# A two-layer hybrid decoder step: the second layer's gates computed step by step inside the first turn of its main block, instead of in a block of their own

## The reference

```python
def c_mixer(h, s_ssm, s_conv, w_in, conv_w, conv_b, dt_bias, a_log, d_skip, norm_w, w_out):
    proj = h @ w_in
    z, xbc, dt = _split(proj, (D_INNER, SSD_CONV_DIM, SSD_HEADS))
    xbc, conv_new = causal_conv(xbc, s_conv, conv_w, conv_b)
    xbc = jax.nn.silu(xbc.astype(F32))
    ...
    dt = jax.nn.softplus(dt.astype(F32) + dt_bias.astype(F32)).reshape(bsz, L, SSD_GROUPS, SSD_HPG)
    a = -jnp.exp(a_log.astype(F32)).reshape(SSD_GROUPS, SSD_HPG)
    y, s_new = ssd_scan(xs, dt, a, bm, cm, s0)      # decays are exp of cumulative sums of dt * a
    y = y + d_skip... * xs
    y = y * jax.nn.silu(z);  y = _rms(y by group) * norm_w;  return y @ w_out, s_new, conv_new
```

## Time and profile before

| | |
|---|---|
| median of 3 runs | 2226.04 us |
| the profiled execution, whole | 2225.12 us |
| its span, first to last instruction | 2223.7 us |
| PE busy | 2101.4 us, 95% of the span |
| DVE busy, ACT busy | 64%, 45% |
| transfers | 436.97 MB, mean 197 GB/s |
| mean granted TensorE clock | 0.975 of full |

### The profile page before, as it was taken

The page is one execution under the profiler, slowest core; times in us unless marked ns, Lnnn a source line. Parts: engine busy times, 40 slices in busy tenths (PEclk is TensorE's granted clock), DMA queues, the critical chain, the costliest instruction groups (busy, mean ns, idle before and its releaser), DMA issues. The chain is left out here.

```text
span 2223.7 us, 41532 instructions
## 1 busy us (share of the span) xinstructions
PE 2101.4 (95%) x15171; PEld 1965.8 (88%) x15171; DVE 1417.5 (64%) x2602; ACT 1006.0 (45%) x1516; POOL 276.9 (12%) x419
## 2 busy tenths in 40 slices
PE   6699999999999999999999599999999999989997
PEld 4599999898989899898999599889888989879996
DVE  4554737475648475585654557787788778875544
ACT  3444444443334343343343346456465475564432
POOL 1100102020101102020100101221211312210000
PEclk8699999999999999999999799999999999999998
DMA  3664667584947758496875175665665766756851
GB/s 96 209 181 139 216 215 261 162 303 145 298 120 222 225 155 283 117 309 209 295 232 183 57 219 171 196 202 175 200 197 171 208 190 186 211 201 193 281 162 68
DMA packets 337147, 436.97 MB, mean 197 GB/s; under 512 B 17644, under 2 KB 296732, under 8 KB 335584
## 3 DMA queue, kind: packets, MB, share of 16 engines
q1 hardware_dynamic: 298672, 298.96, 44.3%
q0 software_dynamic: 38144, 136.48, 18.2%
q10 hardware_dynamic: 224, 0.05, 0.0%
HBM read 355.35 MB, written 80.06 MB: 196 GB/s over the span
## 5 line engine op out<-in xcount | busy, mean ns | idle before, releaser
L145 PE MATMUL bank<-xn_hi,w_hi 128*128 128x288 f32 x3584 | 1079.3, 301 | 35.0 <-ACTq L996 12.3
L146 PE MATMUL bank<-xn_lo,w_hi 128*128 128x288 f32 x3584 | 1060.6, 296 | 0.0
L147 PE MATMUL bank<-xn_hi,w_lo 128*128 128x288 f32 x3584 | 1058.1, 295 | 0.0
L132 DVE TENSOR_TENSOR w_lo<-w_raw,w_hi 128x1024 fp32r<-128x1024 f32 x512 | 624.7, 1224 | 628.3 <-ACT w_hi L126 618.8
L126 ACT ACTIVATE w_hi<-w_raw 128x1024 fp32r<-128x1024 f32 x512 | 541.6, 1060 | 942.1 <-PE bank L147 850.4
L145 PEld LDWEIGHTS bank<-xn_hi,w_hi 128*128 128x128 f32 x3584 | 676.0, 189 | 61.1 <-issue 35.6
L146 PEld LDWEIGHTS bank<-xn_lo,w_hi 128*128 128x128 f32 x3584 | 677.2, 189 | 5.6
L147 PEld LDWEIGHTS bank<-xn_hi,w_lo 128*128 128x128 f32 x3584 | 677.8, 189 | 0.0
L1224 DVE SCALAR_TENSOR_TENSOR state<-state,decay,bank 128x512 f32<-128x512 f32 x128 | 92.1, 740 | 0.0
L1827 POOL DMA_DIRECT2D out_ssm_s<-ssd_state x64 | 48.0, 756 | 305.5 <-DVE ssd_state L2255 242.2
L2094 ACT ACTIVATE ssd_state<-ssd_state,ssd_we 128x128 f32<-128x128 f32 x256 | 82.5, 415 | 0.0
(11 more groups left out here) (441 smaller groups left out, 2339.4 us busy)
## 6 DMA issues: line engine op xcount, KB each, us to landing
w_raw<-in_w_in_ab SPq DMA_DIRECT2D x224, 512.0 KB, 3.8
w_raw<-in_w_in_c SPq DMA_DIRECT2D x128, 512.0 KB, 4.2
w_raw<-in_w_out_ab SPq DMA_DIRECT2D x64, 512.0 KB, 4.7
w_raw<-in_w_out_c SPq DMA_DIRECT2D x64, 512.0 KB, 3.8
state<-in_state_gla POOLq DMA_DIRECT2D x32, 512.0 KB, 9.9
out_gla_s<-state POOLq DMA_DIRECT2D x32, 512.0 KB, 4.2
state<-in_state_mlstm_c POOLq DMA_DIRECT2D x32, 512.0 KB, 10.0
out_mc_s<-state POOLq DMA_DIRECT2D x32, 512.0 KB, 5.4
```

The source lines that it names most:

```text
L132: dve.tensor_tensor(core.w_lo[:, j], core.w_raw[:, j % RAW], core.w_hi[:, j].bitcast(F32), ALU.subtract).then_inc(ws["split"], 1)
L145: pe.matmul(banks[m][:, 0:T], core.w_hi[:, j, kk, col], hi[:, k], start=f, stop=False)
L146: pe.matmul(banks[m][:, 0:T], core.w_hi[:, j, kk, col], lo[:, k], start=False, stop=False)
L147: ins = pe.matmul(banks[m][:, 0:T], core.w_lo[:, j, kk, col], hi[:, k], start=False, stop=e)
```

## The change

The block `gates1` becomes a class `Gates1`, whose methods for each engine are called from the first turn of `ssd_mixer`, one piece per step k. The barrier between the two blocks goes. Its buffers lie over those that only the scan uses (`neg_c`, `decay`, `x_dt_rows`, `cb_masked`, `xbc` and so on; `pad` over later ones), its semaphores are the block's. The two stores to scratch move from SP to POOL, ahead of POOL's first loads, and POOL waits for the stores and for `done` (the end of the gates on DVE) before it loads anything. The product for `dt` goes to bank 4 in place of bank 0, since bank 0 is now filled by the first projection at the same time. The turned `pad` goes to banks 5 and 6 once `hist` says that DVE has read them.

```diff
-            gate_product(pe, core, self.wh, self.wl, B[0][0:64, 0:T], norm.done, self.prod)
+            gate_product(pe, core, self.wh, self.wl, B[4][0:64, 0:T], norm.done, self.prod)
...
+class Gates1:
...
+    def sync(self, sp):
+        sp.dma_start(self.par[:, 0:1], io["ssd_dt_bias"]...).then_inc(self.s_in, 16)
+        sp.dma_start(self.par[:, 1:2], io["ssd_a_log"]...).then_inc(self.s_in, 16)
+        sp.dma_start(self.crow[:], io["state_ssm_conv"][0]...).then_inc(self.r_in, 16)
+    def gpsimd(self, pool):
+        pool.wait_ge(self.nc_d, 1)
+        pool.dma_start(self.scr["negc"], self.au[:]).then_inc(self.saved, 16)
+        pool.wait_ge(self.pad_d, 1)
+        pool.dma_start(self.scr["we"], self.we[:]).then_inc(self.saved, 16)
+        pool.wait_ge(self.saved, 32)
+        pool.wait_ge(self.done, 1)
+    def scalar(self, act, k, st):
+        if k == 0:      # Exp of a_log; Abs, Exp, Ln of the softplus
+        if k == 2:      # Exp of wexp and of we
+    def tensor(self, pe, k):
+        if k == 3:      # pe.wait_ge(self.r_in, 16); the 48 transposes
+        if k == 5:
+            pe.wait_ge(self.pad_d, 1)
+            pe.wait_ge(self.hist, 1)
+            ...         # the 10 transposes
+    def vector(self, dve, k, st):
+        if k is None:   # memset of pad, keep2, dt + bias
+        if k == 1:      # wait_ge(sp_d); softplus, c, negc, arguments of the weights
+        if k == 2:      # five copies to pad
+        if k == 3:      # wait_ge(wx_e); weights, the last slots of pad: pad_d
+        if k == 4:      # wait_ge(turned, 1); three copies to hist: hist
+        if k == 6:      # wait_ge(turned, 2); two copies to cols: done
...
@@ the first turn, engine by engine
         def _(sp):
+            g1.sync(sp)
             load_group(sp, 0)
...
         def _(pool):
+            g1.gpsimd(pool)
             load_nb(pool, 0)
...
                             project_unit(pe, core, ws, gg * SL + (Q_SSD + i), j, ...)
+                            if G is None:
+                                g1.tensor(pe, 4 * i + j)
...
                             split_hi_unit(act, core, ws, gg * SL + (Q_SSD + i + 1), j)
+                            if G is None:
+                                g1.scalar(act, 4 * i + j, st)
                             if j == UNITS - 1:
                                 a_evac(act, gg, i)
...
-            dve.memset(cbm[0:96, 384:416], 0.0)
             dve.memset(cwide[:], 0.0)
-            dve.memset(PP[0:96, :, 384:416], 0.0)
...
+                if G is None:
+                    g1.vector(dve, None, st)
...
                             split_lo_unit(dve, core, ws, gg * SL + (Q_SSD + i + 1), j)
+                        if G is None:
+                            g1.vector(dve, 4 * i + j, st)
+                            if 4 * i + j == 6:
+                                dve.wait_ge(g1.done, 1)
+                                dve.memset(cbm[0:96, 384:416], 0.0)
+                                dve.memset(PP[0:96, :, 384:416], 0.0)
...
-            with nc.cleanup_on_exit():
-                gates1(nc, core, io, scr, g)
             with nc.cleanup_on_exit():
                 ssd_mixer(nc, core, io, out, scr, g, ws)
```

More of the change, by code:

```diff
@@ L1571, in layer1_buffers @@
     return dict(hist=core.sb("ssd_history", [P, CT, 24], F32, ctx), cols=core.sb("ssd_cols", [P, K_N, SSD_H], F32, ctx))
[L1574 to L1616, removed]
@@ new lines, with __init__ @@
+class Gates1:
+    def __init__(self, core, sem, io, scr, g, ctx, gap):
+        self.core, self.io, self.scr, self.g = core, io, scr, g
+        sb = lambda n, s, d=F32: core.sb("g1_" + n, s, d, ctx)
+        self.crow, self.par = sb("conv_rows", [24, 6144]), sb("params", [64, 8])
+        self.dt, self.au, self.c, self.keep2, self.wx = (sb(n, [64, T]) for n in "dt au c keep wexp".split())
+        self.we, self.tot = sb("we", [64, 2 * TS]), sb("total", [64, 8])
+        sb("gap", [P, (gap - 4 * (6144 + 16 + 5 * T + 2 * TS)) // 4])
+        self.pad = sb("pad", [64, K_N * P])
+        (self.s_in, self.r_in, self.u_d, self.sp_d, self.wx_d, self.wx_e, self.pad_d, self.turned, self.nc_d, self.saved, self.hist,
+         self.done) = (sem("g1_" + n) for n in
+                       "small_in rows_in u softplus w_arg w_exp pad turned negc saved hist done".split())
+    def sync(self, sp):
+        io = self.io
+        sp.dma_start(self.par[:, 0:1], io["ssd_dt_bias"].rearrange("o h -> h o")).then_inc(self.s_in, 16)
+        sp.dma_start(self.par[:, 1:2], io["ssd_a_log"].rearrange("o h -> h o")).then_inc(self.s_in, 16)
+        sp.dma_start(self.crow[:], io["state_ssm_conv"][0].rearrange("b t c -> (b t) c")).then_inc(self.r_in, 16)
+    def gpsimd(self, pool):
[7 more added lines that the diff above has]
+        if k == 0:
+            act.wait_ge(self.s_in, 32)
+            act.activation(self.par[:, 1:2], self.par[:, 1:2], ACT.Exp)
+            act.wait_ge(self.u_d, 1)
+            st.then_wait(act.activation(self.au[:], self.dt[:], ACT.Abs))
+            st.then_wait(act.activation(self.au[:], self.au[:], ACT.Exp, scale=-1.0))
+            act.activation(self.au[:], self.au[:], ACT.Ln, bias=1.0).then_inc(self.sp_d, 1)
+        if k == 2:
+            act.wait_ge(self.wx_d, 1)
+            act.activation(self.wx[:], self.wx[:], ACT.Exp)
+            act.activation(self.we[:, TS:2 * TS], self.we[:, TS:2 * TS], ACT.Exp).then_inc(self.wx_e, 1)
+    def tensor(self, pe, k):
+        core, B = self.core, self.core.bank
+        if k == 3:
+            pe.wait_ge(self.r_in, 16)
@@ L1617, in _ @@
             for t in range(CT):
-                i = pe.transpose(core.bank[5 + t // 16][:, 24 * (t % 16):24 * (t % 16) + 24], crow[:, t * P:(t + 1) * P],
+                i = pe.transpose(B[5 + t // 16][:, 24 * (t % 16):24 * (t % 16) + 24], self.crow[:, t * P:(t + 1) * P],
                                  core.ident[0:24, 0:24])
-            i.then_inc(turned, 1)
-            pe.wait_ge(pad_d, 1)
+            i.then_inc(self.turned, 1)
+        if k == 5:
+            pe.wait_ge(self.pad_d, 1)
+            pe.wait_ge(self.hist, 1)
@@ L1622, in _ @@
             for n in range(K_N):
-                i = pe.transpose(core.bank[1 + n // 8][:, 64 * (n % 8):64 * (n % 8) + 64], pad[:, n * P:(n + 1) * P],
+                i = pe.transpose(B[5 + n // 8][:, 64 * (n % 8):64 * (n % 8) + 64], self.pad[:, n * P:(n + 1) * P],
                                  core.ident[0:64, 0:64])
[L1625 to L1629, removed]
+            i.then_inc(self.turned, 1)
+    def vector(self, dve, k, st):
+        core, g, B = self.core, self.g, self.core.bank
+        par, dt, au, c, keep2, wx = self.par, self.dt, self.au, self.c, self.keep2, self.wx
+        pad, we, tot = self.pad, self.we, self.tot
+        cs = samples(c[:, S0:T])
+        if k is None:
@@ L1632, in _ @@
             dve.memset(keep2[:, P:P + 1], 0.0)
-            dve.wait_ge(s_in, 32)
-            dve.tensor_scalar(dt[:], core.bank[0][0:64, 0:T], par[:, 0:1], None, ALU.add).then_inc(u_d, 1)
-            dve.wait_ge(sp_d, 1)
+            dve.wait_ge(self.s_in, 32)
+            dve.tensor_scalar(dt[:], B[4][0:64, 0:T], par[:, 0:1], None, ALU.add).then_inc(self.u_d, 1)
+        if k == 1:
+            dve.wait_ge(self.sp_d, 1)
             st.then_wait(dve.scalar_tensor_tensor(dt[:], dt[:], 0.0, au[:], ALU.max, ALU.add))
@@ L1639, in _ @@
             st.then_wait(dve.tensor_tensor_scan(c[:], keep2[:], c[:], 0.0, ALU.mult, ALU.add))
-            cs = samples(c[:, S0:T])
-            dve.tensor_scalar(negc[:], c[:], -1.0, None, ALU.mult).then_inc(nc_d, 1)
+            dve.tensor_scalar(au[:], c[:], -1.0, None, ALU.mult).then_inc(self.nc_d, 1)
             dve.tensor_scalar(we[:, TS:2 * TS], c[:, S0:T], -1.0, None, ALU.mult)
-            st.then_wait(dve.tensor_tensor(tot[:], c[:, P - 1:P], c[:, TP - 1:TP], ALU.add))
-            dve.tensor_scalar(wx[:, 0:P], c[:, 0:P], tot[:], None, ALU.subtract)
+            st.then_wait(dve.tensor_tensor(tot[:, 0:1], c[:, P - 1:P], c[:, TP - 1:TP], ALU.add))
+            dve.tensor_scalar(wx[:, 0:P], c[:, 0:P], tot[:, 0:1], None, ALU.subtract)
             dve.tensor_scalar(wx[:, P:TP], c[:, P:TP], c[:, TP - 1:TP], None, ALU.subtract)
             dve.tensor_tensor(samples(wx[:, S0:T]), cs, cs[:, :, TD - 1:TD].broadcast_to([64, NB, TD]), ALU.subtract
-                              ).then_inc(wx_d, 1)
+                              ).then_inc(self.wx_d, 1)
+        if k == 2:
             dve.tensor_copy(pad[:, 0:TP], c[:, 0:TP])
@@ L1652, in _ @@
             dve.tensor_copy(pad[:, K_DS * P + 96:K_DS * P + P], dt[:, S0:T])
-            dve.wait_ge(wx_e, 1)
+        if k == 3:
+            dve.wait_ge(self.wx_e, 1)
             dve.tensor_tensor(pad[:, K_W0 * P:K_W0 * P + TP], wx[:, 0:TP], dt[:, 0:TP], ALU.mult)
@@ L1656, in _ @@
                             we[:, TS:2 * TS].unsqueeze(1).broadcast_to([64, 4, TS]))
```

(16 more changed lines are left out.)

## The result

The changed kernel takes 2218.27 us in the median of 8 runs (2215.12 to 2220.33), the kernel before 2226.07 us in 8 runs (2221.7 to 2227.22): ratio 0.9968, 95% interval 0.9957 to 0.9978, so 5 to 10 us faster. I had forecast 2211.1 us and a range up to 2218. The sign was right; the time lies 0.3 us outside the range, and the gain of 7.8 us is little more than half of the 14.0 forecast.

What follows compares the result with a forecast made beforehand. PE, busy 95% of the span, was taken to bound the kernel, with time lost where it stands still or runs slowly. 15.6 + 2.4 + 0.7 − 3.2 − 1.0 − 0.5 = 14.0 us off 2225.1 gave 2211.1 us, range 2208 to 2218.

Steps and rivals of the forecast that it cites:

- The start moves: Layer 1's first projection on PE starts behind the first barrier, at 1254.7 instead of 1270.34 us: gain 15.6 us.
- The clock at the start: PE's first projections run at 2.4 GHz after a short pause, instead of 4.9 us at half rate: gain 2.4 us.
- The wait for weights: PE's first-turn wait for late quad 1 weights goes, as POOL's loads no longer compete then: gain 0.7 us.
- the hidden chain of the gates: Gates' work on ACT and DVE completes the slot array near 1275 us, before PE wants it at 1276.6: no cost.
- The transposes: The 48 and 10 transposes now stand between PE's projections, at full clock: cost 3.2 us, or 6.6 at the other end.
- Rival A: The clock falls at the transposes, slowing them and 4.9 us of products: 5.6 us more, 2216.7 us; chance 0.17.
- The wait for the history: At step 5 PE waits for DVE's copies of the turned rows: cost 1.0 us, between 0.5 and 3.
- POOL's burst moves: POOL's 3.41 MB of loads move onto the weights of quads 3 and 4, mostly covered by reserve: cost 0.5 us.
- rival B: POOL's burst starves the weights, so PE waits 6 us in quads 3 and 4: 2216.6 us; chance 0.12.
- D: Weights stay late round after round, two rounds costing 16.2 us: 2226.8 us, slower than before; chance 0.03.
- The sign that I had named for a wrong forecast: The second turn, forecast to begin near 1324.5 us, begins later than 1329, or later turns grow.

Runs made afterwards that it cites:

- e2: Changed kernel with the 48 transposes split into three parts of 16 behind the third, fourth and fifth projection units; 2216.36 us, ratio to before 0.9962.
- e1: Changed kernel with POOL's two halves of state loads held until PE has used the first turn's third and fourth quads; 2212.29 us, ratio to before 0.9948.
- e9: Changed kernel with PE's turning of the convolution tails one unit later, steps 15 and 17, in every turn; 2217.82 us, ratio to before 0.9965.
- e5: Changed kernel with both halves of the state loads paced and the 48 transposes in thirds; 2209.2 us, ratio to before 0.9933.
- e4: Kernel before the change, with both halves of the first group's state loads paced by two waits; 2222.03 us, ratio to before 0.9987.
- e7: Changed kernel with only the second half of the state loads held, until PE has used the fourth quad; 2211.5 us, ratio to before 0.9947.
- e6: e5 with the 10 transposes of the padded slots, and DVE's copies and memsets for them, one step later; 2211.38 us, ratio to before 0.9935.

## Why the prediction was half right

By its own steps, with the measured value in place of the term:

- **The start moves**, 15.6 us: 17.3 − 1.5 = 15.8 us. Right.
- **The clock at the start**, 2.4 us: 1.00 from the first product on (1253 to 1268 us). Right.
- **The wait for weights** of 0.7 us: gone. Right, as is the hidden chain of the gates: the slot array was complete at 1273.6 us, 21.4 us behind PE's start, and PE waited for the history, not for it.
- **The transposes**, −3.2 us: 3.2 for the 48 and 0.7 for the 10, −3.9. The 48 ran at full clock themselves, 3.1 us from 1265.2 to the next product at 1268.3, against 5.3. A little more than half, so the term was small by 0.7.
- **Rival A** was half right, and I gave it 0.17. The clock fell behind them: stretches of 2 us with means 0.84, 0.50 and 0.81 make 3.4 us at half rate, 1.7 us lost, where the rival had 2.4 for the clock and 3.2 for slow transposes. e2 shows the cause, for thirds of them keep 1.00, and all five profiles of whole pieces without a wait behind them show the fall. The sentence of the Trainium skill (TensorE: Matmul & The Clock Gate, Part 4: PE-mode transpose), that transposes don't count as activity in the same way, agrees with this fall; that the fast clock doesn't engage for them, taken literally, does not, since they ran at 1.00 for 3.1 us. The weight I took from an idle PE that kept its clock for longer was misplaced, and I had its own row of transposes at 0.50 as a warning.
- **The wait for the history**, −1.0 us: 0.8. Right.
- **POOL's burst moves**, −0.5 us: this step failed. e1 against the changed kernel gives 77.3 − 71.5 = 5.8 us in the turn, and the third fall of the clock, behind the wait for x, lies in the second turn: 6 us at a mean of 0.72 are 3.4 us at half rate, 1.7 us more. Together −7.5 us by the profiles; the runs' ratios give 4.5 with wide intervals.

Three things were wrong in that step. The latest landing was 16.2 us, not at most the 10.5 us allowed: I set the shortage of bytes against the reserve, but under the burst four units were under way at once, where I had counted on one or two (rivals B and D), and the earlier trace rows already showed a landing of 18.6 us. Then I looked for the cost where PE waits for weights. PE never did; ACT and DVE, one quad ahead, took the lateness of 16.2 − 10.5 = 5.7 us, and behind the late split stood the 20.8 us of convolution that had no reserve even before. Its row was there: the x transposes at 1338.55 us, which PE reached just when DVE was done. At last, the wait for x cost another 1.7 us of half clock, which rival B had left out; the half clock behind the wait for the tails cost nothing of its own (e9). Rival B, with 0.12, had the mechanism and nearly the size (6 us), at the wrong engine.

The sign that I had named for a wrong forecast came: the second turn began at 1329.6, later than 1329. One reading of the earlier trace rows was off as well, without effect on the sum: the 0.7 us for `ssd_z` stand at 1340.3, in the second turn.

Sum: 15.8 + 2.4 + 0.7 − 3.9 − 1.7 − 0.8 − 7.5 = 5.0 us. The spans of the two profiles differ by 7.3 us, of which 1253.1 − 1250.7 = 2.4 us lie ahead of the change, in code that is the same; the remaining 4.9 agree. The runs' 5 to 10 us hold it. With the burst paced and the transposes split (e5) the gain is 12 to 18 us by its interval, and 15.8 + 68.2 − 70.5 = 13.5 by the profile; the 14.0 of the forecast fit that kernel, not the one that was forecast.

## What to carry to other kernels

When a step is overlapped with the next, list what was behind it in every queue and ask what its late start now falls on: here 3.4 MB of loads that cost the kernel before 1.1 us (e4) cost half the gain behind an earlier start, and two waits that pace them gave most of it back in the turn. Look for the cost not where the resource is used but where its delay comes out, by following the helper engine's queue to the next thing that the bound engine needs, and measure the reserve of that chain before the change. Price a wait of PE of 2 us with the products at half clock behind it, unless PE would next stand waiting for the same late chain anyway.

## What the runs showed of the hardware

- 48 transposes in one piece, 3.1 us amid products, were followed by a fall of the granted clock to 1.2 GHz, between 0.5 us before the next product (e7) and about 1.3 us behind its start (e9); 16 at a time were not (e2, e5, e6).
- PE kept 2.4 GHz over 1.5 us without work at the block's start, over the 0.8 us before the ten transposes, over 1.2 and 1.4 us before the tails (second profile of the changed kernel, e2) and over the 1.6 us of e7, but not over the 2.1 us before L2001 or L1922, nor over 3.6 and 4.5 us (e2, e9).
- A weight unit of 512 KB, landed in 3.9 us in the median, needs up to 16.2 us beside 3.4 MB from another queue and up to 13.4 beside 2.4 MB, although beside the 3.4 MB the weights' queue still has 39.8% of the transfer engines' time. The Trainium skill (DMA: Bandwidth & Descriptors, Queues, rings and completion order) has the engines take turns between queues; the shares of 53.9% and 39.8% fit that roughly, and tell nothing of the latency of a single transfer.
- The time up to the end of the product for `dt`, in code that no version changed, varied by up to 7.6 us between profiles (1247.8 to 1255.4 us).
